# Tiling the opening's modulation on TensorE, moving layer 1's gate, and projecting last by token tiles

## The reference

```python
def _adaln(cond, w, b):
    m = jax.nn.silu(cond) @ w + b
    shift, scale, gate = jnp.split(m, 3, axis=-1)
    return shift[:, None, :], scale[:, None, :], gate[:, None, :]

def _trunk(x, cond, shift_fn, init_fwd, init_bwd, P):
    for i in range(DEPTH):                      # DEPTH = 2
        shift, scale, gate = _adaln(cond, P["ada_w"][i], P["ada_b"][i])
        h = _rms_norm(x, P["norm_pre"][i]) * (1.0 + scale) + shift
        # i == 0: out = _hyena_mixer(h, P, 0), which ends in  y @ hy_w_out + hy_b_out
        # i == 1: out = _rwkv_mixer(...), which ends in  y @ rw_w_o
        x = x + gate * _rms_norm(out, P["norm_post"][i])
```

## Time and profile before

| | |
|---|---|
| device time, three runs | 3078.47 us median (3074.14 to 3084.37) |
| the profiled execution | 3078.53 us, span 3076.9 us, so 1.6 us lie outside the span |
| PE busy | 2724.8 us, 89% of the span |
| DVE, ACT, POOL busy | 47%, 24%, 8% |
| mean granted TensorE clock | 0.945 of full speed |
| DMA | 242.61 MB moved, 79 GB/s on average |

### The profile page before, as it was taken

How to read it: one execution, slowest core, us unless ns; L and a number is a source line. 1 busy time by engine, 2 the same in 40 slices (tenths; PEclk the granted TensorE clock), 3 DMA queues, 4 the chain that set the end, 5 groups by cost and what they waited for, 6 DMA issues and landing times. The chain is left out here.

```text
span 3076.9 us, 74252 instructions
## 1 busy us (share of the span) xinstructions
PE 2724.8 (89%) x33434; PEld 1683.3 (55%) x33434; DVE 1445.2 (47%) x2147; ACT 741.0 (24%) x1281; POOL 259.8 (8%) x416
## 2 busy tenths in 40 slices
PE   6999999989999689769999999578888889887697
PEld 1555555543444344245555555367777777777543
DVE  2222222239999900240000000488998989988102
ACT  2212122122121100210000011344544445453100
POOL 1000000000000000000000000011221112111100
PEclk9999999989999899889999999689999999999698
DMA  5232232342231064223232222101111111110231
GB/s 191 70 90 87 80 91 82 90 135 69 69 103 51 17 248 165 89 63 100 89 100 89 93 91 86 43 25 39 42 40 31 41 39 35 48 30 27 85 130 59
DMA packets 211452, 242.61 MB, mean 79 GB/s; under 512 B 22848, under 2 KB 158352, under 8 KB 210029
## 3 DMA queue, kind: packets, MB, share of 16 engines
q1 hardware_dynamic: 199338, 196.03, 20.1%
q0 software_dynamic: 11200, 42.21, 3.7%
q10 hardware_dynamic: 644, 0.24, 0.0%
HBM read 184.95 MB, written 53.49 MB: 77 GB/s over the span
## 5 line engine op out<-in xcount | busy, mean ns | idle before, releaser
L105 PE MATMUL ps<-mix,rw 128*128 128x512 f32 (+1 forms) x2048 | 564.5, 439 | 20.6 <-DMA rw<-in_rw_w_v 5.2
L105 PE MATMUL ps<-hT,hw 128*128 128x512 f32 (+1 forms) x2048 | 561.0, 435 | 5.5 <-ACT hT L119 5.5
L105 PEld LDWEIGHTS ps<-mix,rw 128*128 128x128 f32 x2048 | 313.9, 194 | 271.1 <-issue 271.1
L105 PEld LDWEIGHTS ps<-hT,hw 128*128 128x128 f32 x2048 | 312.5, 191 | 251.2 <-issue 251.2
L105 PE MATMUL ps<-ow,oy 128*128 128x512 f32 x640 | 279.7, 600 | 22.0 <-DMA oy<-scratch_y_d 18.7
L1555 POOL TENSOR_SCALAR e_Sd<-e_S,e_pcd 128x64 f32<-128x64 f32 x256 | 159.9, 641 | 780.3 <-DVE e_S L108 316.3
L105 PEld LDWEIGHTS ps<-ow,oy 128*128 128x128 f32 x640 | 122.9, 193 | 177.8 <-issue 158.5
L119 ACT ACT_TABLE_LOAD x90 | 115.5, 1283 | 282.7 <-PE ps L105 272.7
L108 DVE SCALAR_TENSOR_TENSOR mix<-xx,col,hT 128x640 f32<-128x640 f32 x48 | 38.7, 880 | 286.5 <-PE ps L105 286.4
L113 DVE TENSOR_SCALAR hcv<-hpad,hpc 128x641 f32<-128x641 f32 x48 | 29.6, 616 | 300.5 <-ACT hpad L119 300.5
L116 DVE TENSOR_TENSOR rout<-ps,rsig 128x640 f32<-128x640 f32 x16 | 13.2, 825 | 275.0 <-ACT rsig L119 275.0
(11 more groups left out here) (237 smaller groups left out, 4121.5 us busy)
## 6 DMA issues: line engine op xcount, KB each, us to landing
hw<-in_hy_w_in SPq DMA_DIRECT2D x64, 512.0 KB, 3.9
scratch_rkvz_d<-rout POOLq DMA_DIRECT2D x64, 320.0 KB, 3.2
aw<-in_ada_w SPq DMA_DIRECT2D x32, 512.0 KB, 5.3
scratch_vx_d<-hot POOLq DMA_DIRECT2D x32, 320.0 KB, 3.1
conv_room<-scratch_vx_d SPq DMA_DIRECT2D x8, 1280.0 KB, 9.2
aw<-in_ada_w SPq DMA_DIRECT2D x8, 1024.0 KB, 16.9
ow<-in_hy_w_out SPq DMA_DIRECT2D x32, 256.0 KB, 3.2
rw<-in_rw_w_r SPq DMA_DIRECT2D x16, 512.0 KB, 3.7
```

Of the source, the lines that this page charges most:

```text
L105: return nc.tensor.matmul(out, lhsT, rhs, start=first, stop=last)
```

## The change

Four things change, one in each of four places.

1. In the opening a weights step runs as four tiles of 64 rows by half of the columns. The bias row has a tile of its own (`abrow`), and the two row halves' sums are kept apart in PSUM until ACT copies one and DVE adds the other. `ORDER` is new, ACT issues `frow` before `feats` and `fw` and does the first sigmoid between them, `cols` is copied after `argument(0)`, and the 1 MB table is loaded at the end of `hyena_in` instead.
2. `out_proj` for layer 0 loses `modulation(3)`, its eight weight loads, its copies, POOL's products and the store.
3. Both output projections get y in eight transfers (four of one block, four of three), issued by ACT's queue ahead of its other work.
4. Layer 1's projection becomes a function of its own, `last_proj`. Its second half goes token tile by token tile, with all 16 blocks of weights held in SBUF (`f_w2`), and layer 1's gate is computed between its second and third tile (`GATE_AT = 2`).

```diff
@@ startup
-    ORDER = ["cond", "cols", "fcols", "F0", "bias", "a0", "a1", "x0", "F1", "a2", "x1", "a3", "x2", "a4", "x3", "x4", "a5", "x5", "F2",
-             "a6", "x6", "x7", "a7", "shift", "scale"]
+    ORDER = ["cond", "fcols", "F0", "bias", "a0", "cols", "a1", "x0", "x1", "F1", "x2", "a2", "x3", "x4", "a3", "x5", "x6", "a4", "x7", "F2",
+             "a5", "a6", "a7", "shift", "scale"]
+    ROWS = (slice(0, 2), slice(64, 66))
...
-                sp.dma_start(tab[:, P:TAB_N], A["tab"][:, P:TAB_N]).then_inc(s_tab, 16)
-                sp.wait_ge(s_tab, 16)
...
                 sine(0)
                 channels(0)
+                channels(1)
                 sine(1)
-                for k in range(1, 6):
+                for k in range(2, KD):
                     channels(k)
                 sine(2)
-                for k in range(6, KD):
-                    channels(k)
                 a.wait_ge(pe_.sem, pe_.now("a7"))
-                ac_.did(act(mrow[:, D:2 * D], ps[0:2, 2:4, :].rearrange("p b n -> p (b n)"), ACT.Copy), "scale row")
+                for c, at in enumerate(ROWS):
+                    ac_.did(act(mrow[at, :], ps[at, 0:2, :].rearrange("p b n -> p (b n)"), ACT.Copy), ("half row", c))
...
                     pe.wait_ge(s_aw[k], 16)
-                    for b in range(4):
-                        last = mm(ps[0:2, b, :], condT[:, k:16:KD], aw[:, k, b * 512:(b + 1) * 512], False, k == KD - 1)
+                    for q in range(2):
+                        for half in range(2):
+                            rows = slice(64 * half, 64 * half + 64)
+                            for c, at in enumerate(ROWS):
+                                block = aw[rows, k, (2 * c + q) * 512:(2 * c + q + 1) * 512]
+                                last = mm(ps[at, 2 * half + q, :], condT[rows, k:16:KD], block, half == 1 and k == 0, k == KD - 1)
...
-                dv_.did(nc.vector.tensor_copy(mrow[:, 0:D], ps[0:2, 0:2, :].rearrange("p b n -> p (b n)")), "shift row")
+                for c, at in enumerate(ROWS):
+                    v.wait_ge(ac_.sem, ac_.now(("half row", c)))
+                    dv_.did(tt(mrow[at, :], mrow[at, :], ps[at, 2:4, :].rearrange("p b n -> p (b n)"), ADD), ("row", c))
@@ FirstLoads.start, run by SP at the end of hyena_in
         self.filters(sp, A, 0)
+        sp.dma_start(tab[:, P:TAB_N], A["tab"][:, P:TAB_N]).then_inc(self.sems["tab"], 16)
         sp.dma_start(self.dft[:, :], A["dft"]).then_inc(self.sems["dft"], 16)
@@ out_proj, now for layer 0 alone
-    PARTS = ((0, 2), (1, 0), (1, 1), (1, 2)) if l == 0 else ()
+    PARTS = ((0, 2), (1, 0), (1, 1)) if l == 0 else ((1, 2),)
...
-        Y_PARTS = [slice(0, 1), slice(1, 4), slice(4, 8), slice(8, 12), slice(12, KE)]
+        Y_PARTS = [slice(k, k + 1) for k in range(4)] + [slice(k, k + 3) for k in range(4, KE, 3)]
...
                     modulation(2)
                     columns(1)
                     columns(2)
-                    modulation(3)
...
+                y_v = A["y_d"].rearrange("(k p) t -> p k t", p=P)
+                for n, ks in enumerate(Y_PARTS):
+                    a.dma_start(y[:, ks, :], y_v[:, ks, :]).then_inc(s_y[n], 16)
+                part_rows(0)
@@ last_proj, tensor
+                for j in range(NT):
+                    if j == GATE_AT:
+                        modulation()
+                    pe.wait_ge(dv_.sem, dv_.now(("first", j)))
+                    for k in range(KE):
+                        if j == 0 and k % 4 == 0:
+                            pe.wait_ge(s_w2[k // 4], 64)
+                        last = mm(ps[:, j, :], y[:, k, j * P:(j + 1) * P], w2[:, k, :], k == 0, k == KE - 1)
+                    pe_.did(last, ("tile", j))
@@ last_proj, vector
+                for j in range(NT):
+                    dv_.did(nc.vector.tensor_copy(o[:, j, first], ps[:, j, :]), ("first", j))
+                v.wait_ge(ac_.sem, ac_.now(("ss", 0, NT - 1)))
+                dv_.did(ts(ss[:, 0, :], ss[:, 0, :], 1.0 / D, EPS, MUL, ADD), "part_var")
+                v.wait_ge(s_x, 16)
+                v.wait_ge(s_g, 32)
+                for j in range(NT):
+                    dv_.did(tt(o[:, j, first], o[:, j, first], gate[:, j // 4, first], MUL), ("gated", j))
+                for j in range(NT):
+                    v.wait_ge(ac_.sem, ac_.now(("ss", 1, j)))
+                    v.wait_ge(dv_.sem, dv_.now("part_var"))
+                    dv_.did(ts(rs[:, j:j + 1], ss[:, 1, j:j + 1], 1.0 / D, ss[:, 0, j:j + 1], MUL, ADD), ("var", j))
+                    dv_.did(tt(o[:, j, second], ps[:, j, :], gate[:, j // 4, second], MUL))
+                    v.wait_ge(ac_.sem, ac_.now(("std", j)))
+                    dv_.did(nc.vector.reciprocal(rs[:, j:j + 1], rs[:, j:j + 1]))
+                    v.wait_ge(dv_.sem, dv_.here())
+                    dv_.did(stt(x[:, j, :], o[:, j, :], rs[:, j:j + 1], x[:, j, :], MUL, ADD), ("x", j))
@@ last_proj, scalar, behind the eight loads of y and the squares of the first half
+                for j in range(NT):
+                    if j == GATE_AT:
+                        a.wait_ge(pe_.sem, pe_.now("part"))
+                        for r in range(2):
+                            for rows in ROWS:
+                                ac_.did(act(part[rows, r, :], ps[rows, 5 + r, :], ACT.Copy), "part")
+                        for n in range(GATE_AT):
+                            std(n)
+                    a.wait_ge(pe_.sem, pe_.now(("tile", j)))
+                    a.wait_ge(ac_.sem, ac_.here())
+                    ac_.did(act(sq[:, :], ps[:, j, :], ACT.Square, accum_out=ss[:, 1, j:j + 1]), ("ss", 1, j))
+                    if j >= GATE_AT:
+                        std(j)
```

More of the change, by code:

```diff
@@ L298, in turn_row @@
                 def turn_row(n):
-                    if n == 0:
-                        pe.wait_ge(ac_.sem, ac_.now(("h", KD - 1)))
-                        pe.wait_ge(dv_.sem, dv_.now("shift row"))
-                    else:
-                        pe.wait_ge(ac_.sem, ac_.now("scale row"))
-                    for j in range(8 * n, 8 * n + 8):
-                        last = nc.tensor.transpose(ps[:, 4 + n, 2 * j:2 * j + 2], mrow[:, j * P:(j + 1) * P], ident[0:2, 0:2])
+                    pe.wait_ge(ac_.sem, ac_.now(("h", KD - 1)))
+                    pe.wait_ge(dv_.sem, dv_.now(("row", n)))
+                    for j in range(KD):
+                        last = nc.tensor.transpose(ps[:, 4 + n, 2 * j:2 * j + 2], mrow[ROWS[n], j * P:(j + 1) * P], ident[ROWS[n], ROWS[n]])
                     return last
@@ L1158, in part_rows @@
                         for rows in ROWS:
-                            a.wait_ge(po_.sem, po_.now(("sum", 0, rows.start)))
+                            a.wait_ge(po_.sem, po_.now(("sum", rows.start)))
                     for r in range(2):
```

244 lines of the change are left out of this document (162 added, 82 removed).

## The result

The changed kernel takes 3043.01 us (median of four runs, 3039.35 to 3046.34), the kernel before 3081.26 on the same chip (four runs, 3074.14 to 3084.37). The ratio is 0.9875, with a 95% interval of 0.9854 to 0.9896: 38.5 us less, and between 32 and 45. Forecast was 3039.2 with a range of 3030 to 3054, and 39.3 us less.

What follows compares the result with a forecast made beforehand. It took PE's list to bound the opening, the late gate to hold up the first projection's end, and squares, norms and stores the last tail. From 3078.53, -20.3 - 11.4 - 7.6 = -39.3 gave 3039.2 us, range 3030 to 3054.

Steps and rivals of the forecast that it cites:

- Late gate: End of first projection: without layer 1's gate, load_norm's first ACT work starts at about 1277.2, not 1297.48; 20.3 us gained.
- The gate in the last stage: Last projection: the gate's modulation between two token tiles costs PE 7.9 us; its tail is hidden beside matmuls.
- Gap: Last projection, between PE's halves: PE resumes after one bank is copied, not five; 3.27 becomes about 0.85, 2.4 us gained.
- Tail: Last projection, PE's last matmul to the end: only one tile left, 6.1 us against 22.97; 16.9 us gained.
- Eight transfers of y: Both output projections: loading y on ScalarE's queue changes 0 us, with -1 and +2 as bounds.
- The table: End of hyena_in: the added 1 MB load, estimated at 3.6 us, is hidden under 20 us of cover; 0 us.
- The opening: Start to hyena_in: shorter weights steps and a new order start hyena_in at 65.9 instead of 73.48; 7.6 us gained.
- the walk: Opening: step-by-step timing of PE's new order from F0 at 19.8, ending at 64.6 before 0.35 meeting and 1 us clock allowance.
- The rival of the low clock: Opening: PE at half pace from x0 on, 6.3 us lost instead of 7.6 gained, 3053.1 us; chance 0.12.
- The rival of early loads: Opening: the filter's weights land at 14 instead of 19, the walk moves forward by 5.5, 3033.7 us; chance 0.12.
- Not overlapping tiles: Opening: the four tiles run without overlap, a weights step takes 6.9 instead of 1.76, total 3077 us; chance 0.02.
- one bank in a row: Last projection, second half: 32 records into one bank take 0.86 us each instead of 0.43, 3108 us; chance 0.02.

Runs made afterwards that it cites:

- the old order: The changed kernel with layer 1's last projection in two halves of 512 columns, all five tiles after each, gate computed between them: 3058.03 us, ratio 0.9928.
- the run of the old opening: The changed kernel with the opening's two-tile weights steps, table load, load order and PE order put back as before: 3048.8 us, ratio 0.9892.
- the better opening: The changed kernel with filter loads first on SyncE's queue, a weights chunk after each x step from x2, F2 after a4, ACT reordered: 3023.63 us, ratio 0.9807.
- two chunks ahead: The changed kernel with weights chunks a2 and a3 moved ahead of x0 in PE's opening order, later chunks drawn forward: 3045.03 us, one run.

## Why the prediction was right, and where it wasn't

- **Late gate, -20.3**: right, in size and in reason. The pair of profiles gives -20.33, the run that puts the gate back 20.35. ACT starts 0.66 us after DVE's last operation began. The forecast had the store of the last tile and DVE's last operation end together at about 1277, and they do so at 1270.0; which of them the stage waits for stays open.
- **The gate in the last stage, +7.9, its tail hidden**: right. 2997.24 - 2989.31 = 7.93, and the gate is there 14.85 us after, where 28 was the bound; DVE is idle again before the fourth tile.
- **Gap, -2.4**: right, 3.27 became 0.79. The run of the old order adds that this gain isn't apart from the gate's: in the old order the modulation fills the gap by itself.
- **Tail, -16.9**: right, 22.97 became 5.99, -17.0; the old order gives 22.95 back.
- **Eight transfers of y, 0**: right within its bounds of -1 and +2: nothing in the first projection. In the last, the first matmul comes 0.48 us later after the first issue and the first half takes 0.81 more (71.81 against 71.00). These 1.3 us are nearly all that lies between the -10.0 of this pair and the -11.4 forecast; whether the transfers or the execution brought them isn't shown.
- **The table, 0**: right, see the run of the old opening.
- **The opening, -7.6**: the size holds (-7.95 in the first pair; two profiles of the old opening start hyena_in at 73.48 and 74.40, four of the new at 67.0 in the mean: -6.9), but one step of it failed. "1 us for what the clock may lose in the wait" was put on the wait behind a2, the one that the walk named. The walk also has a1 ending at 32.5 and x0 starting at 35.0, and that gap of 2.5 us I passed over. There the clock fell, in all four executions. Where it fell once, part of the lost time went into the wait behind a2: hyena_in came at 65.53 and 66.22, against 64.95 by the walk with the blocks' meeting. Where it fell twice, hyena_in came at 67.65 and 68.68. If all that lies above the walk is put down to the clock, the term is 0.6 to 3.7 us and not 1; that the first pair gave 7.95 for a forecast of 7.6 is in part luck.
- **The rival of the low clock (3053.1, 0.12)** was half right: the clock falls, but doesn't stay down from x0 on, since it is back at 1.00 by 46 (in two of the four executions it falls once more). Its reason, taken from the rule on transposes in the Trainium skill (TensorE: Matmul & The Clock Gate, Part 4: PE-mode transpose), is not what the runs show: with all eight x steps in it, the better opening held 1.00, and its x steps took 0.77 us each.
- **The rival of early loads (3033.7, 0.12)** didn't happen, and for the reason given against it: F0 at 19.74. That I found "nothing but the new order" for it was right for this change. But the remedy was one step further: the loads at the head of the other queue have landed by 7.8.
- **Not overlapping tiles, one bank in a row (0.02 each)** fell: a chunk of 16 records takes 1.78 us, and the 96 records of token tiles 41.47, 0.43 each.
- **The base**: 3.8 us between 3039.2 and 3043.01 are 2.8 of the kernel before, whose median was 3078.47 in the first runs and 3081.26 in all four, and 1 of the change.

## What to carry to other kernels

When you walk an engine's list by hand, write down every gap, also those that only follow from two start times, and ask of each what it does to the clock behind it, not only what it costs itself. An order can be dense in the sum and still lose: put the long independent chunks ahead of each chain of short dependent steps, and move a chunk only after looking where the hole goes. Look too at which engine the next block waits for: with two chunks ahead PE was done 2.6 us earlier, and the block began no sooner. And ask what starts the walk: the seven loads that held it back were small and had only to stand ahead of large ones.

## What was not expected of the hardware

- TensorE's granted clock fell from 1.00 to 0.50 (2.4 to 1.2 GHz) behind short idle times: ahead of x0 after 1.22, 1.60, 2.34, 2.55, 2.90 and twice 2.94 us, each with 0.79 or 0.80 us between x0 and x1 (after the 2.34 it was down when x0 began). With 0 and 0.27 us ahead of x0 it held. Gaps of 0.79 alone between dense pieces never made it fall, in the old opening or the new, and neither did the 1.48 us ahead of x7 in both profiles of the old one.
- Further on the length of the gap doesn't decide. Ahead of x3, with 0.80 us behind it, 0.93, 1.67 and 1.79 us did no harm, and 1.15, 1.17, 1.44 and 3.18 were followed by a second fall. What else decides there stays open; the same code fell a second time in two of four executions.
- rwkv_scan took from 948.0 to 959.0 us with the same code, more than the rest of the program varies. A profile of one execution tells a difference of under 10 us only stage by stage. What varies in it was not looked into.
